# The gating unit of a two-block transformer kernel: order of head preparation, mixing and the split of the gated activations

## What is computed

```
z = gelu(h @ w_in);  u, v = split(z, 2)          # w_in: 1024 x 2048
v = layernorm(v, g, b)
v = v.reshape(chunk 8, s 128, head 8, c 128)
ws = where(tril(128 x 128), w_s, 0)              # one 128 x 128 matrix per head
mixed = einsum('hts,bnshc->bnthc', ws, v) + b_s
gated = u * mixed
x = x + g1 * (gated @ w_out)                     # w_out: 1024 x 1024
```

## Time and profile before

| | |
|---|---|
| median of 3 runs | 2693.25 us (2692.01 to 2693.99) |
| the profiled execution: its time | 2691.99 us |
| the profiled execution: its span | 2690.2 us |
| busy share of the span: PE, DVE, ACT, POOL | 97%, 51%, 34%, 11% |
| mean granted TensorE clock | 0.98 of full |
| chain of work that ended last, by engine | PE 89%, DVE 4%, issue 3%, POOL 2%, DMA 1%, ACT 1% |

### The profile page before, as it was taken

The page is one execution under the profiler, slowest core; times in us unless marked ns, Lnnn a source line. Parts: engine busy times, 40 slices in busy tenths (PEclk is TensorE's granted clock), DMA queues, the critical chain, the costliest instruction groups (busy, mean ns, idle before and its releaser), DMA issues.

```text
span 2690.2 us, 33642 instructions
## 1 busy us (share of the span) xinstructions
PE 2603.1 (97%) x12080; PEld 2097.4 (78%) x12080; DVE 1364.3 (51%) x2123; ACT 911.9 (34%) x1423; POOL 285.0 (11%) x278
## 2 busy tenths in 40 slices
PE   8999999999999999899999999999999999998988
PEld 2478888888888788777888888888878897886676
DVE  2765555545454533444344443435551224998963
ACT  2442222222222322333222222222322124887741
POOL 2110000000002000010000000000010002556621
PEclk9999999999999999899999999999999999999998
DMA  8712323232200810321111111110324463346521
GB/s 302 235 63 79 109 78 109 78 109 78 78 32 37 230 28 1 125 79 50 45 62 34 59 47 47 47 47 0 110 90 122 141 151 80 95 105 158 164 79 63
DMA packets 177425, 245.20 MB, mean 91 GB/s; under 512 B 55728, under 2 KB 132656, under 8 KB 177328
## 3 DMA queue, kind: packets, MB, share of 16 engines
q1 hardware_dynamic: 177328, 243.92, 29.1%
HBM read 210.33 MB, written 39.58 MB: 93 GB/s over the span
## 4 chain that ended last, share of the span: by engine, by line
PE 89%; DVE 4%; issue 3%; POOL 2%; DMA 1%; ACT 1%; DVEq 0%; POOLq 0%; ACTq 0%; SPq 0%
PE banks L1673 23%; PE banks L1675 23%; PE banks L1674 23%; PE banks L1762 3%; PE banks L2070 3%; PE banks L2052 3%; DVE Hlo L1349 1%; PE banks L2040 1%; PE banks L2039 1%; PE banks L1893 1%; PE banks L1892 1%; PE banks L1894 1%; PE banks L1703 1%; DMA stage<-ada_w 1%; POOL SUM L790 1%
## 5 line engine op out<-in xcount | busy, mean ns | idle before, releaser
L1673 PE MATMUL banks<-Hhi,Whi 128*128 128x512 f32 x1792 | 711.7, 397 | 15.2 <-ACT TB L1038 7.1
L1674 PE MATMUL banks<-Hlo,Whi 128*128 128x512 f32 x1792 | 704.0, 393 | 0.0
L1675 PE MATMUL banks<-Hhi,Wlo 128*128 128x512 f32 x1792 | 703.3, 392 | 0.0
L1397 DVE SCALAR_TENSOR_TENSOR X<-banks,mod,X 128x512 f32<-128x512 f32 x512 | 380.9, 749 | 208.6 <-PE banks L1675 206.2
L1673 PEld LDWEIGHTS banks<-Hhi,Whi 128*128 128x128 f32 x1792 | 341.1, 190 | 91.8 <-ACT TB L1038 7.9
L1673 PE MATMUL banks<-Mhi,Whi 128*128 128x512 f32 x1024 | 400.9, 392 | 0.0
L1675 PE MATMUL banks<-Mhi,Wlo 128*128 128x512 f32 x1024 | 399.4, 390 | 0.0
L1674 PE MATMUL banks<-Mlo,Whi 128*128 128x512 f32 x1024 | 399.3, 390 | 0.0
L1674 PEld LDWEIGHTS banks<-Hlo,Whi 128*128 128x128 f32 x1792 | 340.8, 190 | 72.1 <-issue 2.2
L1675 PEld LDWEIGHTS banks<-Hhi,Wlo 128*128 128x128 f32 x1792 | 340.4, 190 | 72.4
L913 ACT ACTIVATE Whi<-stage 128x2048 fp32r<-128x2048 f32 x93 | 177.4, 1908 | 554.2 <-PE banks L1675 539.2
(11 more groups left out here) (168 smaller groups left out, 2696.6 us busy)
## 6 DMA issues: line engine op xcount, KB each, us to landing
stage<-w SPq DMA_DIRECT2D x64, 1024.0 KB, 5.6
stage<-ada_w SPq DMA_DIRECT2D x48, 1024.0 KB, 5.4
stage<-w_in SPq DMA_DIRECT2D x13, 1024.0 KB, 6.9
stage<-sgu_in SPq DMA_DIRECT2D x8, 1024.0 KB, 6.7
x_saved<-X SPq DMA_DIRECT2D x16, 512.0 KB, 2.6
X<-x_saved SPq DMA_DIRECT2D x16, 512.0 KB, 6.7
QS<-q_heads SPq DMA_DIRECT2D x32, 256.0 KB, 4.4
KH<-k_heads SPq DMA_DIRECT2D x32, 256.0 KB, 5.3
```

The costliest lines, as they stand in the source:

```text
L1397: nc.vector.scalar_tensor_tensor(out=X[:, k, half(hf)], in0=Dn[:, i % D_BANKS, :], scalar=gate[:, k:k + 1], in1=X[:, k, half(hf)], op0=ALU ...
L1673: nc.tensor.matmul(out_bank, whi, xhi, start=start, stop=False)
L1674: nc.tensor.matmul(out_bank, whi, xlo, start=False, stop=False)
L1675: return nc.tensor.matmul(out_bank, wlo, xhi, start=False, stop=stop)
```

## The change

Four edits in the gating unit.

1. `prepare(j)` moves ahead of the gates step j, and `mix(j)` follows right behind the gates of the same j. ACT's part for j = 0 is put inside the first gates step, between its second and third gelu; DVE's part for j = 0 stands ahead of the split of the next weight unit.
2. ACT's `resplit` of the gating unit no longer waits for all of `X` to be gated: each piece waits for the mix of its own tile. (For the second `resplit` of the program nothing changes.)
3. DVE splits six of the eight tiles of the first half inside `mix(3)`, two behind each of the first three products with `X`, by the new function `lower_half`.
4. SP's reload of the residual moves from `resplit` into the first `project` step, and there it stands behind the load of a second w_out unit instead of ahead of it.

```diff
         do["normalise_v"](T)
         for j in range(4):
-            step("gates", src_in(sgu_in, j + 1) if j < 3 else src_in(sgu_out, 0), dict(a=4), j)
-            if j > 0:
-                mix(j - 1)
-
             do["prepare"](T, j)
             T.add(h=4)
-        mix(3)
+            step("gates", src_in(sgu_in, j + 1) if j < 3 else src_in(sgu_out, 0), dict(a=4), j)
+            mix(j)
         do["resplit"](T)
...
             def resplit(T):
+                if T("sp") == 2:
+                    x_again(T)
+
+            def project(T, j, gate, first, then=None):
+                if first and T("sp") == 1:
+                    x_again(T, -2 * KT)
+
+            def x_again(T, since=0):
 
                 sync.wait_ge(x_stored, 16 * KT * T("sp"))
                 for k in range(KT):
-                    sync.wait_ge(lo_done, T("h", KT + k + 1))
+                    sync.wait_ge(lo_done, T("h", KT + k + 1 + since))
                     sync.dma_start(X[:, k, :], x_saved[k * P:(k + 1) * P, :]).then_inc(x_back_first if k < FT else x_back, 16)
...
                         i = hf * FT + f
+                        if j == 0 and i == 2:
+                            upper_half(T, 0)
                         act.wait_ge(a_ready, T("a", i + 1))
...
             def prepare(T, j):
+                if j > 0:
+                    upper_half(T, j)
+
+            def upper_half(T, j):
 
                 act.wait_ge(v_norm, 2)
                 act.wait_ge(ws_masked, KT)
...
             def resplit(T):
                 if T("v") > 0:
                     act.wait_ge(mixed_done, T("vg"))
-                act.wait_ge(d_free, T("d"))
+                    act.wait_ge(d_free, T("d"))
                 act.wait_ge(a_ready, T("a"))
                 for hf in range(NH):
                     for k in range(KT):
+                        if T("v") == 0:
+                            act.wait_ge(d_free, T("d", 4 * (k // 2) + 2 * (k % 2) + hf + 1 - 2 * KT))
                         nc.scalar.activation(Hhi[:, k, half(hf)], X[:, k, half(hf)], ACT.Copy).then_inc(hi_done, 1)
...
                         nc.vector.tensor_tensor(X[:, head, half(hf)], bank, X[:, head, half(hf)],
                                                 ALU.mult).then_inc(d_free, 1)
+                        if j == 3 and i < 3:
+                            for k in (2 * i, 2 * i + 1):
+                                lower_half(T, 0, k)
...
-                    for k in range(KT):
-                        dve.wait_ge(hi_done, T("h", hf * KT + k + 1))
-                        nc.vector.tensor_tensor(Hlo[:, k, half(hf)], X[:, k, half(hf)],
-                                                Hhi[:, k, half(hf)].bitcast(F32), ALU.subtract).then_inc(lo_done, 1)
+                    for k in range(6 if T("sp") == 1 and hf == 0 else 0, KT):
+                        lower_half(T, hf, k)
```

More of the change, by code:

```diff
@@ L762, in _ @@
                             split=load, norm_pool=norm_pool, spill=spill, values=values, gates=gates,
-                            resplit=resplit, spatial=spatial, rotation=rotation, finish=finish,
+                            resplit=resplit, project=project, spatial=spatial, rotation=rotation, finish=finish,
                             heads=heads, vals=vals, plain=plain, attend_start=attend_start, attend=attend))
@@ L1469, in resplit, with lower_half @@
                         first_rstd(T, hf)
-                    for k in range(KT):
-                        dve.wait_ge(hi_done, T("h", hf * KT + k + 1))
-                        nc.vector.tensor_tensor(Hlo[:, k, half(hf)], X[:, k, half(hf)],
-                                                Hhi[:, k, half(hf)].bitcast(F32), ALU.subtract).then_inc(lo_done, 1)
+                    for k in range(6 if T("sp") == 1 and hf == 0 else 0, KT):
+                        lower_half(T, hf, k)
+            def lower_half(T, hf, k):
+                dve.wait_ge(hi_done, T("h", hf * KT + k + 1))
+                nc.vector.tensor_tensor(Hlo[:, k, half(hf)], X[:, k, half(hf)],
+                                        Hhi[:, k, half(hf)].bitcast(F32), ALU.subtract).then_inc(lo_done, 1)
             def first_rstd(T, hf):
```

## The result

| | before | changed |
|---|---|---|
| median, 5 runs each | 2693.25 us (2691.99 to 2694.20) | 2677.77 us (2671.23 to 2680.40) |
| ratio to before, 95% interval | | 0.9944 (0.9926 to 0.9961) |
| profiled execution: time, span | 2691.99, 2690.2 | 2671.23, 2669.4 |
| the gating unit in it (measured as below) | 154.13 | 137.98 |

A forecast was written before the change was run, and what follows sets the result against it. PE's work, busy 97% of the span, was taken as the bound. Six loss terms of 18.28 us less 2.2 of new waits gave 16.1 off 2691.99, 2675.9; with the median 1.26 higher, 2677.1 us, range 2673.8 to 2682.5.

The forecast's parts named there:

- Heads ahead of their gates: Last mix: heads split during the last gates, so the 3.23 us wait and 4.98 us at half clock go, 8.2 us.
- the two terms: Last mix: 3.23 us of PE waiting for the halves of heads 6 and 7, and 4.98 us at clock 0.50.
- the wait for a bank: Second projection step: PE waits 3.56 us for a bank to be emptied, held up by the late weight load; it goes.
- Two new waits: Start of the projection: PE waits 0.90 us at k = 4 and 1.26 at k = 6, 2.2 us replacing 3.26.
- The clock under two short stops: First projection group: clock stays up at no cost; the rival, a falling clock, gave 2678.7 to 2682.1 us, chance 0.15.
- The row of the norm: Next norm: 16 matmuls in 5.5 us with three 0.35 us stops at clock 1.00, evidence that short stops cost nothing.
- The rule of the Trainium skill: Projection start: a PE idling briefly between matmul groups often enough swings its clock between two levels, so the start runs slow.
- Reload behind a weight load: Second projection step: weight unit issued at 990.8, ahead of the reload, so 3.56 us of wait and 1.67 behind it go.
- Sum: Whole change: 18.28 us of loss less 2.2 of new waits gives 16.1 us; forecast median 2677.1 us.
- The slower rival: All four mixes: heads not ready when their gates end, 23 us more, 2716 us; chance 0.02.
- their four terms: Last mix and second projection step: 3.23 and 4.98 us, then 3.56 for the bank and 1.67 at half clock, all go.
- 1.58 us of slow start: First projection step: starts at half clock, 23.45 us instead of 21.87; goes if the short stops leave the clock up.

The follow-up runs named there:

- heads_late: Changed kernel with each pair of heads prepared behind its gates instead of ahead, mix right behind its gates; unit 173.50 us, median 2713.06 us.
- two_tiles_first: Changed kernel with DVE's last mix taking tiles 0 and 2 and the first-half Hlo before tiles 1 and 3; unit 135.94 us, median 2676.19 us.
- order_split: Changed kernel with the residual's reload put back ahead of the second w_out unit's load; unit 145.72 us, median 2686.43 us.
- no_interleave: Changed kernel without the Hlo splits inside the last mix, ACT still copying tile by tile; unit 140.96 us, second profile 141.05, median 2680.21 us.
- reload_only: Kernel before with only the residual's reload moved behind the second w_out unit's load; unit 149.66 us, median 2690.18 us.
- order_reload: Kernel before with heads prepared ahead of their gates and the reload behind the weight load, no split tile by tile; unit 142.15 us, median 2681.65 us.
- order_only: Kernel before with only the heads prepared ahead of their gates and mixed right behind them; unit 144.39 us, median 2686.30 us.

## Why the prediction came out as it did

The time and the mechanism were right. By its own steps:

- **Heads ahead of their gates.** Right. No wait on `Vlo`, the last mix in 5.31 us at 1.00. Shown by edit 1 alone, which holds both, and from the other side by `heads_late`, which brings the waits back four times. Its size alone, 9.7 against 8.2, is no error of the two terms: it shortened the wait for a bank and took the slow start behind it.
- **Two new waits.** Forecast 0.90 and 1.26 us at k = 4 and k = 6; measured 0.79 and 1.20 there, with the slower first matmul behind each. The first projection step took 23.93 us (1079.36 to 1103.29), 2.06 over 21.87; forecast 24.1. `two_tiles_first` shows their cause, DVE's order, by removing it.
- **The clock under two short stops.** Taken at no cost, and 1.00 in all three profiles of the change and in `order_split`. This was the largest open risk. The row of the norm pointed the right way, but its stops were 0.35 us long and these 0.52 and 0.93, so that it carried over was in part luck: one stop of 2.42 us at the same place did bring the clock down (`no_interleave`). The rule of the Trainium skill (page "TensorE: Matmul & The Clock Gate", section "A second HAM failure mode: psum-queue depth-cycling") that the prediction sets against it does not show here with its two stops; it speaks of frequent ones, and of that two stops are no test.
- **Reload behind a weight load.** Right, by `reload_only` and by the profile after. The first load was issued at 988.4 (forecast 990.8, in a run in which all lies 2.2 us earlier), the reload at 1086.7 (1088.7), `Wlo` ended at 1093.0 (1095.3), the reload's last tile landed within 9.9 us (10.3).
- **Sum.** 16.15 us of unit time against 16.1; the median 2677.77 against 2677.1. The first agreement is that of the mechanism. The second is closer than the runs can tell, with five of them 9.2 us apart.
- **The slower rival.** Its condition never arose. Made to happen, its mechanism holds, and its price is 19.4 us (173.50 - 154.13 by the units; 2713.06 us against 2693.5 for before in the same series by the medians gives 19.6) where the prediction has 23. The prediction adds the 2.2 us of the two short stops to it; behind a mix at half clock these do not occur.

Two things in the working were too simple, though both left the sum alone. The terms were written as if each belonged to one edit, and **they do not add**: alone, edits 1 and 4 give 9.7 and 4.5 us and together 12.0; edits 2 and 3 lose 1.3 behind edit 1 (by the units; nothing by the medians) but win 4.2 once edit 4 is in. What ties them is first the load: as long as the late weight unit sets the second projection step, whatever PE wins in the first turns into waiting, and whatever it loses there is hidden. Second, the slow start varies: edits 1 and 4 together miss the 13.4 us of their four terms mostly because the projection started with 2.85 us lost in place of 1.58. The change takes all of the loss but the two stops, and no slow start is left in it to vary, which is why the sum came out.

And the **1.58 us of slow start** is no fixed price. It was used for a term that goes, which was right: in the kernel before, the load ends the wait for a bank, so what a slow start takes more, that wait takes less. But it was the lowest of those measured at this place: the same start cost 2.3 and 2.9 us in the two profiles of edit 1 alone, 2.4 with edit 4 alone, 2.5 in `no_interleave` and 2.85 in `order_reload`. Edits 2 and 3 therefore win 4.2 us (142.15 to 137.98), where the terms say 3.26 + 1.58 - 2.2 = 2.6.

What stays open: why whole runs of one kernel spread by several microseconds while the unit does not. In the profiles the difference lies ahead of the unit (its first gelu starts between 976.4 and 982.8) and behind it. Ahead of it, where all these kernels have the same code, the trace tells what differs: PE's busy time with the same 4109 matmuls goes from 952.2 us (the first profile of the change) over 954.7 (the kernel before) to 960.6 (`order_only`), and in the first 200 us of the span the clock averages 0.96, 0.94 and 0.91. So it is more or less time at half clock; why it is longer in one execution than in another, nothing here was made to find.

## What to carry to other kernels

Where the busiest engine stands at 97%, list what it loses around one stage as a sum, wait by wait with the clock behind each, and ask of each wait what is late next: here a load behind a queue of transfers took back all that an earlier start had won, until it was moved. Order the side engines' work by what the bound engine wants next, not by tile number: two short stops of up to a microsecond kept the clock, one of 2.4 us at the same place doubled its cost. To judge a change of a fifth of a per cent, time the stage inside the trace: it repeated within 0.1 us where runs of the same kernels spread by 4 to 9.

## What the runs showed of the hardware that was not expected

- **The length of a stop alone does not set the clock.** One of 2.42 us behind the small matmuls of the mix was followed by 0.50 in two of two profiles. Stops of 2.54 and 1.9 us behind 128x512 matmuls (the wait for a bank, two profiles of edit 1 alone) left 1.00. Those of 3.40 and 5.7 us at the same place left 0.54 and 0.53. That the matmuls ahead of the stop make the difference is not shown: no run changes them alone.
- **The clock can fall behind a wait.** In `heads_late` it was 1.00 through the first 3.1 us of idle time and fell about 1 us after PE had gone on; so again behind the second and the fourth (1.5 and 0.8 us), while the third mix had half clock from its start.
- **A slow start differs in length.** Over the first 6 us of the projection, behind a wait of 3.2 us each time, the clock averaged 0.50 in `order_reload`, 0.59 and 0.50 in the two profiles of edit 1 alone, 0.58 in `reload_only` and 0.72 in the kernel before. Two profiles of one kernel differ, and so do two kernels (before and `reload_only`) whose PE came from half clock alike. What sets it the runs don't tell.
- **Two matmul sizes at half clock.** The mix at 0.50 ran all its 10.29 us without the clock rising. In every profile it rose during the 128x512 matmuls behind a mix or a wait, between 2.7 and 6.1 us after their start.
